# Sharing the low-part subtraction of the split weights between VectorE and GpSimd in a two-block kernel

## The chip, the cores and the metric

The kernel runs on one core of one Trainium2 chip. The metric is device time in microseconds (us) from start to end of one execution. A core has TensorE (PE, matmul), VectorE (DVE), ScalarE (ACT), GpSimd (POOL) and SyncE (SP); here SP only issues the weight transfers.

## The reference

Two transformer-like blocks run over 256 tokens of width 2048, all in float32. The first has a pooling mixer, a gated linear recurrence (RG-LRU) and a product-key expert layer (PEER: 8 heads, top 16 of 128 x 128 experts, gathered rows of `peer_u` and `peer_v`). The second has a stick-breaking attention, a causal depthwise convolution of 31 taps, two gates and an MLP with squared ReLU. Cut to the products that carry the time:

```python
# first block
proj = rmsnorm(x) @ w_in;  y = [pool_mixer(proj), rg_lru(proj)];  h = x + y @ w_out
s1, s2 = q @ keys1.T, q @ keys2.T;  expert = top16 of top16(s1) + top16(s2);  gate = softmax
h = h + sum_k gate_k * gelu(peer_u[expert_k] . z) * peer_v[expert_k]
# second block
q, k, v, glu_a, glu_b, g1, g2 = split(rmsnorm(x) @ w_in_2 + b_in_2)
merged = sigmoid(g1) * (attention(q, k, v) @ w_sb) + sigmoid(g2) * (conv(glu) @ w_cv)
x = x + rmsnorm(merged @ w_o)
x = x + rmsnorm(square(relu(rmsnorm(x) @ w_up)) @ w_down)
```

The expert layer is computed densely: all 16384 rows of `peer_u` and `peer_v` are multiplied, in 8 chunks, and a gate matrix made with one-hot products picks the experts that count.

## The kernel before

**Products in split form.** Every weight product keeps float32 accuracy by splitting both operands into a high part (rounded to fp32r, the fast type of TensorE) and a low part (the rest). The activations stand in `ZA` or `ZB` with 512 columns: 256 high and 256 low. A weight tile of 128 x 128 takes two matmuls: `hi` times all 512 columns, and `lo` times the first 256.

**Units and halves.** The work is a list of `N` = 544 units u. A unit is one block of 128 output rows against 2048 inputs (16 weight tiles), and it comes in two halves of 8 tiles (512 KB of weights each): 1088 halves h, in the order of `HALVES`. The stages by unit number: 0 to 39 the mixer projections (`lx`, `pl`, `gt`, `ot`), 40 to 55 the query product (`wq`), from `UB[0]` = 56 to 311 the expert chunks (`u` and `v`), from `F0` = 312 the second block's projections with attention and convolution between them, 352 to 383 gates, 384 to 399 merge, 400 to 415 output, and from `M0` = 416 the MLP (`up`, `dn`).

**The path of a half.** SP loads it into one of three buffers `raw` (line 338). ACT rounds it into one of five buffers `hi` (line 615). DVE subtracts, `lo = raw - hi`, over 128 x 1024 elements (line 978). PE waits for `lo` and runs 16 matmuls (lines 386 and 387). SP may load the next half into a `raw` buffer when the subtraction that read it is done; this is a wait on `s_lo` in `sync_program`. On PE the wait is `weights_ready`.

**Order on each engine.** ACT, DVE and POOL run the same function `walk(u, evac, prep)` for each unit: `evac` handles the results of the unit before in up to three parts, and between the parts `prep` handles the two halves 2u+3 and 2u+4. On ACT `prep` is the rounding and on DVE the subtraction. On POOL `prep` is an empty function. Each engine runs its program in the written order, so a wait in it holds all that stands behind it.

**Evacuation.** ACT copies the low half of a result out of PSUM (line 622), DVE adds the two halves (`join`, line 984), and POOL scales by the norm (line 1451) or adds a residual (lines 1491, 1524). `join` has one input in PSUM and one in SBUF. The subtraction of line 978 has two inputs in SBUF.

**What runs between.** In units 42 to 59 DVE searches the top 16 (`MAX8`, `MATCH_REPLACE8`, `FIND_INDEX8`). In units 61 to 72 it decodes and picks indices (lines 1211, 1220, 1229), with half of each pick on POOL (line 1587). In units 67 to 82 it makes the one-hot matrices `oneB` and `oneA` (lines 1253, 1255), four per unit; ACT scales half of each `oneB` by the gate (line 787), POOL the other half (line 1595), and PE multiplies them (line 474). In units 314 to 366 DVE runs 248 convolution taps, five per unit (lines 1271 and 1274; two SBUF inputs for most), beside four attention groups whose mask products are on POOL (lines 1621 and 1628).

## Time and profile before

| | us |
|---|---|
| median of 3 runs (3285.91 to 3322.47) | 3305.0 |
| the profiled execution, its own time | 3285.91 |
| its span from first to last instruction | 3283.7 |
| PE busy | 3173.8 |
| DVE busy | 2180.9 |
| ACT busy | 1690.9 |
| POOL busy | 876.5 |

The profile is one execution. Busy time of an engine is the union of its instructions; an instruction that is held up after its start by another engine's use of a shared resource still shows as busy. A timeline row gives start, duration, engine, line, operation, shapes and count; a bracket gives the idle time before it and what ended it. The line numbers are those of the kernel before.

### The profile page before, as it was taken

The numbers are of one execution on the slowest core, as the hardware profiler recorded it, in microseconds if no ns is written. First come the engines' busy times: TensorE is split into PE (matmuls) and PEld (weight loads), VectorE is DVE, ScalarE is ACT, GpSimd is POOL, SyncE is SP. The second block draws the span as 40 slices with busy tenths as digits, with TensorE's granted clock in tenths as the row PEclk, the third lists the DMA queues.
The fourth block names the chain that finished last, engine by engine and source line by source line (L and its number), as shares of the span: only waits on it lengthen the run. The fifth ranks groups of instructions, "written<-read, shape, count | busy, mean of one in ns | idle before, by whom it ended". The sixth has DMA issues, their size and how long they took to land.

```text
span 3283.7 us, 46918 instructions
## 1 busy us (share of the span) xinstructions
PE 3173.8 (97%) x18206; PEld 2776.8 (85%) x18206; DVE 2180.9 (66%) x2875; ACT 1690.9 (51%) x2618; POOL 876.5 (27%) x808
## 2 busy tenths in 40 slices
PE   7999989999999999999999999999998999999997
PEld 6788878888888888888888877888887788888886
DVE  7857998764656555565656579898666855555555
ACT  5554456544545444454545645555656444444454
POOL 2332444531313222231313434323242000000003
PEclk9999999999999999999999999999999999999999
DMA  6465556666666666665666655455665556666664
GB/s 206 144 207 181 167 157 222 226 203 206 188 216 188 217 192 214 190 213 192 212 194 190 187 159 154 154 165 188 187 191 161 158 189 188 190 192 190 190 187 139
DMA packets 177708, 615.35 MB, mean 187 GB/s; under 512 B 18128, under 2 KB 34896, under 8 KB 176080
## 3 DMA queue, kind: packets, MB, share of 16 engines
q1 hardware_dynamic: 157824, 572.59, 55.6%
q10 hardware_dynamic: 19664, 39.76, 3.4%
q8 instruction: 145, 2.38, 0.3%
q14 instruction: 75, 0.61, 0.0%
HBM read 593.41 MB, written 18.87 MB: 186 GB/s over the span
## 4 chain that ended last, share of the span: by engine, by line
PE 73%; DVE 17%; issue 4%; ACT 3%; POOL 2%; DMA 1%; ACTq 0%; POOLq 0%; DVEq 0%
PE G L386 47%; PE G L387 24%; DVE lo L978 7%; DVE CV L1274 2%; DVE oneB L1253 1%; ACT hi L615 1%; POOL tS L1451 1%; DVE tS L984 1%; DVE oneA L1255 1%; ACT oneB L787 0%; DMA raw<-in_pu 0%; DVE ZA L1297 0%; DMA raw<-in_w_in 0%; POOL X L1471 0%; ACT tA L622 0%
## 5 line engine op out<-in xcount | busy, mean ns | idle before, releaser
L386 PE MATMUL G<-ZA,hi 128*128 128x512 f32 x5120 | 1812.5, 398 | 44.0 <-DVE lo L978 26.5
L978 DVE TENSOR_TENSOR lo<-raw,hi 128x1024 fp32r<-128x1024 f32 x1088 | 1429.4, 1333 | 343.0 <-ACT hi L615 342.4
L387 PE MATMUL G<-ZA,lo 128*128 128x256 f32 x5120 | 1435.0, 280 | 0.0
L386 PE MATMUL G<-ZB,hi 128*128 128x512 f32 x3584 | 1250.9, 394 | 5.2 <-DVE ZB L1262 5.2
L615 ACT ACTIVATE hi<-raw 128x1024 fp32r<-128x1024 f32 x1088 | 1119.2, 1052 | 210.0 <-DMA raw<-in_w_in 99.6
L386 PEld LDWEIGHTS G<-ZA,hi 128*128 128x128 f32 x5120 | 966.9, 189 | 271.9 <-DVE lo L978 33.7
L387 PE MATMUL G<-ZB,lo 128*128 128x256 f32 x3584 | 1003.4, 280 | 0.0
L387 PEld LDWEIGHTS G<-ZA,lo 128*128 128x128 f32 x5120 | 972.7, 190 | 0.5
L386 PEld LDWEIGHTS G<-ZB,hi 128*128 128x128 f32 x3584 | 673.1, 188 | 158.7 <-issue 3.5
L387 PEld LDWEIGHTS G<-ZB,lo 128*128 128x128 f32 x3584 | 678.4, 189 | 0.0
L622 ACT ACTIVATE tA<-G 128x256 f32<-128x256 f32 x560 | 212.8, 380 | 898.0 <-PE G L387 893.1
L1451 POOL TENSOR_TENSOR tS<-tS,R 128x256 f32<-128x256 f32 x224 | 258.0, 1152 | 694.5 <-DVE tS L984 694.5
L984 DVE TENSOR_TENSOR tS<-G,tA 128x256 f32<-128x256 f32 x336 | 141.4, 421 | 254.7 <-ACT tA L622 242.0
L1491 POOL TENSOR_TENSOR tA<-tA,X 128x256 f32<-128x256 f32 x128 | 104.9, 819 | 545.8 <-ACT tA L622 545.8
L984 DVE TENSOR_TENSOR X<-G,tA 128x256 f32<-128x256 f32 x128 | 54.4, 425 | 273.0 <-POOL tA L1491 273.0
L1524 POOL TENSOR_TENSOR tA<-tA,Y 128x256 f32<-128x256 f32 x48 | 35.4, 738 | 612.9 <-ACT tA L622 612.9
L984 DVE TENSOR_TENSOR Y<-G,tA 128x256 f32<-128x256 f32 x80 | 34.0, 425 | 168.1 <-POOL tA L1524 128.3
L1487 POOL TENSOR_TENSOR tS<-tS,Gc 128x256 f32<-128x256 f32 x96 | 123.4, 1285 | 50.9 <-ACT tS L655 50.9
L1274 DVE SCALAR_TENSOR_TENSOR CV<-UC,col,CV 128x256 f32<-128x256 f32 x240 | 123.0, 513 | 6.9
L1595 POOL TENSOR_TENSOR oneB<-oneB,IJG 128x512 f32<-128x512 f32 x32 | 62.6, 1956 | 79.6 <-DVE oneB L1253 79.6
L474 PE MATMUL M<-oneB,oneA 128*128 128x128 f32 x512 | 66.9, 286 | 15.7 <-DVE oneA L1255 14.0
L474 PEld LDWEIGHTS M<-oneB,oneA 128*128 128x128 f32 x512 | 62.9, 200 | 20.9 <-DVE oneA L1255 18.3
(263 smaller groups left out, 1375.4 us busy)
## 6 DMA issues: line engine op xcount, KB each, us to landing
raw<-in_pu SPq DMA_DIRECT2D x256, 512.0 KB, 4.1
raw<-in_pv SPq DMA_DIRECT2D x256, 512.0 KB, 4.2
raw<-in_w_in SPq DMA_DIRECT2D x192, 512.0 KB, 3.9
raw<-in_w_up SPq DMA_DIRECT2D x128, 512.0 KB, 4.1
raw<-in_w_down SPq DMA_DIRECT2D x128, 512.0 KB, 4.0
raw<-in_w_out SPq DMA_DIRECT2D x32, 512.0 KB, 4.2
raw<-in_wq SPq DMA_DIRECT2D x32, 512.0 KB, 3.9
g_scratch<-stage ACTq DMA_DIRECT2D x16, 1024.0 KB, 7.1
```

The costliest lines, as they stand in the source:

```text
L386: pe.matmul(G[:, 0:512], hi[w][:, k % 8, :], Z[:, k, :], start=first, stop=False, skip_group_check=True)
L387: m = pe.matmul(G[:, 0:256], lo[w][:, k % 8, :], Z[:, k, 0:256], start=False, stop=last, skip_group_check=True)
L474: t = pe.matmul(M[:, 128 * n:128 * n + 128], oA[k % 2][:, 4 * v + n, :], oB[k % 2][:, 4 * v + n, :], start=True, stop=True, skip_group_che ...
L615: act.activation(hi[w][:, :, :], raw[r][:, :].rearrange("p (k n) -> p k n", k=8), ACT.Copy).then_inc(s_hi, 1)
L622: act.activation(tA[b % 3][:, :], GB[b % 4][:, 256:512], ACT.Copy).then_inc(s_low, 1)
L978: dve.tensor_tensor(lo[w][:, :, :], raw[r][:, :].rearrange("p (k n) -> p k n", k=8), hi[w][:, :, :].bitcast(F32), ALU.subtract).then_inc(s ...
L984: dve.tensor_tensor(dst, GB[b % 4][:, 0:256], tA[b % 3][:, :], ALU.add).then_inc(s_join, 1)
L1274: dve.scalar_tensor_tensor(out=CV[:, j, :], in0=b[:, k:k + 256], scalar=w, in1=CV[:, j, :], op0=ALU.mult, op1=ALU.add).then_inc(s_dw, 1)
L1451: pool.tensor_tensor(b, b, R[:, :], ALU.mult).then_inc(s_scl, 1)
L1487: pool.tensor_tensor(b[:, :], b[:, :], Gc[:, :, i], ALU.mult).then_inc(s_gm2, 1)
L1491: pool.tensor_tensor(t[:, :], t[:, :], X[:, i, :], ALU.add).then_inc(s_vx, 1)
L1595: pool.tensor_tensor(oB[k % 2][:, 4:8, :], oB[k % 2][:, 4:8, :], IJG[:, 2, 8 * k + 4:8 * k + 8].unsqueeze(2).broadcast_to([128, 4, 128]), ...
```

## The change

A function `pool_part(h)` says how many of the 8 weight tiles of half h have their low part computed on POOL: 0 for the units 0 to 2, 5 for the units 42 to 59, 4 for the units 60, 61 and 67 to 83, 7 for half 2*M0+3, and 2 for all other halves. POOL takes the last tiles (`c` to 8), DVE the first. A new semaphore `s_lop` counts POOL's parts, and `POOL_SPLITS[h]` is its count after half h. PE waits for both parts before a half's matmuls, and SP waits for both before it loads over a `raw` buffer. The empty `prep` of POOL's `walk` becomes a real one, so POOL's subtractions stand in its program where DVE's stand in DVE's. Two halves at the border M0 are called from POOL's `evac` and from its mixing loop.

```diff
+def pool_part(h):
+    u = h // 2
+    if h == 2 * M0 + 3:
+        return 7
+    if u < 3:
+        return 0
+    if 42 <= u < UB[0] + 4:
+        return 5
+    if UB[0] + 6 <= u < UB[0] + 11:
+        return 2
+    return 4 if UB[0] + 4 <= u < UB[0] + 28 else 2
+POOL_SPLITS = [sum(pool_part(i) > 0 for i in range(h + 1)) for h in range(NH)]
@@ sync_program
                 if h >= NRAW:
                     sp_.wait_ge(s_lo, h - NRAW + 1)
+                    if POOL_SPLITS[h - NRAW]:
+                        sp_.wait_ge(s_lop, POOL_SPLITS[h - NRAW])
@@ tensor_program
             def weights_ready(h):
                 pe.wait_ge(s_lo, h + 1)
+                if POOL_SPLITS[h]:
+                    pe.wait_ge(s_lop, POOL_SPLITS[h])
@@ vector_program
             def prep(h):
-                r, w = h % NRAW, h % NW
+                r, w, c = h % NRAW, h % NW, 8 - pool_part(h)
                 dve.wait_ge(s_hi, h + 1)
-                dve.tensor_tensor(lo[w][:, :, :], raw[r][:, :].rearrange("p (k n) -> p k n", k=8),
-                                  hi[w][:, :, :].bitcast(F32), ALU.subtract).then_inc(s_lo, 1)
+                dve.tensor_tensor(lo[w][:, 0:c, :], raw[r][:, 0:128 * c].rearrange("p (k n) -> p k n", k=c),
+                                  hi[w][:, 0:c, :].bitcast(F32), ALU.subtract).then_inc(s_lo, 1)
@@ pool_program
+            def prep(h):
+                r, w, c = h % NRAW, h % NW, 8 - pool_part(h)
+                if c < 8:
+                    pool.wait_ge(s_hi, h + 1)
+                    pool.tensor_tensor(lo[w][:, c:8, :], raw[r][:, 128 * c:1024].rearrange("p (k n) -> p k n", k=8 - c),
+                                       hi[w][:, c:8, :].bitcast(F32), ALU.subtract).then_inc(s_lop, 1)
@@ pool_program, evac, before the part of "yo"
+                if u == M0 - 1 and part == 1:
+                    prep(2 * M0 + 3)
@@ pool_program, in the loop over MIX_POOL
+                        if n == 6:
+                            prep(2 * M0 + 4)
@@ pool_program, main loop
+            for h in range(3):
+                prep(h)
             for u in range(N + 1):
-                walk(u, evac, lambda h: None)
+                walk(u, evac, prep)
```

## Rows read from the trace of the kernel before

**Rows 1.** The page: span, and busy time of each engine.
```profile
span 3283.7 us, 46918 instructions
PE 3173.8 (97%) x18206; PEld 2776.8 (85%) x18206; DVE 2180.9 (66%) x2875; ACT 1690.9 (51%) x2618; POOL 876.5 (27%) x808
```

**Rows 2.** Busy time by stretch: stretch, its length, then each engine.
```profile
92.00:150.00 58.00, 51.90 (x276) 44.12 (x275) 52.08 (x70) 30.11 (x49) 25.13 (x17) 0.97 0.43 135
...
390.00:444.00 54.00, 49.20 (x271) 41.97 (x270) 48.31 (x71) 25.43 (x41) 20.32 (x17) 0.97 0.53 161
444.00:604.00 160.00, 145.52 (x965) 131.22 (x964) 144.56 (x113) 105.09 (x242) 81.38 (x49) 0.97 0.62 198
...
740.00:1891.00 1151.00, 1151.00 (x6631) 1010.53 (x6630) 654.36 (x732) 581.54 (x873) 310.51 (x331) 1.00 0.63 200
1891.00:2256.00 365.00, 344.66 (x1921) 297.86 (x1920) 317.31 (x452) 197.73 (x276) 128.62 (x89) 0.98 0.52 161
...
2612.00:3258.00 646.00, 646.00 (x3714) 569.36 (x3714) 359.29 (x463) 299.30 (x431) 51.07 (x61) 1.00 0.60 188
```

**Rows 3.** Waits of PE: who waited for whom, total us, times, longest.
```profile
PE G L386 <- DVE lo L978: 26.5, 14, 10.7
PE M L474 <- DVE oneA L1255: 14.0, 7, 3.3
```

**Rows 4.** Groups of DVE by form: busy us, mean ns of one, idle before.
```profile
L978 DVE TENSOR_TENSOR lo<-raw,hi 128x1024 fp32r<-128x1024 f32 x1088 | 1429.4, 1333 | 343.0 <-ACT hi L615 342.4
...
L1065 DVE TENSOR_TENSOR ZA<-tS,ZA 128x256 fp32r<-128x256 f32 x16 | 6.6, 411 | 0.0
```

**Rows 5.** Timeline of DVE and POOL in the expert stage, steady part.
```profile
1202.81 1.38 DVE L978 TENSOR_TENSOR lo<-raw,hi 128x1024 fp32r<-128x1024 f32 x1 [0.52 <-ACT hi L615]
1204.55 1.45 DVE L978 TENSOR_TENSOR lo<-raw,hi 128x1024 fp32r<-128x1024 f32 x1 [0.36 <-ACT hi L615]
...
1202.37 0.74 POOL L1451 TENSOR_TENSOR tS<-tS,R 128x256 f32<-128x256 f32 x1 [3.00 <-DVE tS L984]
1203.64 1.28 POOL L1487 TENSOR_TENSOR tS<-tS,Gc 128x256 f32<-128x256 f32 x1 [0.53 <-ACT tS L655]
```

**Rows 6.** Timeline of DVE: two subtractions in a row, free and behind POOL.
```profile
387.67 2.36 DVE L978 TENSOR_TENSOR lo<-raw,hi 128x1024 fp32r<-128x1024 f32 x2
...
462.51 4.78 DVE L978 TENSOR_TENSOR lo<-raw,hi 128x1024 fp32r<-128x1024 f32 x2 [0.46 <-ACT hi L615]
```

**Rows 7.** Timeline of one unit in the one-hot stage, DVE, ACT, POOL.
```profile
551.28 2.58 DVE L978 TENSOR_TENSOR lo<-raw,hi 128x1024 fp32r<-128x1024 f32 x2 [0.46 <-ACT hi L615]
553.78 1.21 DVE L1253 TENSOR_TENSOR oneB<-con,IJG 128x1024 f32<-128x1024 f32 x1
...
556.05 2.06 DVE L1253 TENSOR_TENSOR oneB<-con,IJG 128x1024 f32<-128x1024 f32 x1
...
560.68 2.58 DVE L978 TENSOR_TENSOR lo<-raw,hi 128x1024 fp32r<-128x1024 f32 x2 [0.46 <-ACT hi L615]
...
558.14 0.41 ACT L787 ACTIVATE oneB<-oneB,IJG 128x128 f32<-128x128 f32 x1 [1.83 <-DVE oneB L1253]
...
559.34 0.36 ACT L622 ACTIVATE tA<-G 128x256 f32<-128x256 f32 x1
559.60 2.00 ACT L615 ACTIVATE hi<-raw 128x1024 fp32r<-128x1024 f32 x2
...
555.07 1.96 POOL L1595 TENSOR_TENSOR oneB<-oneB,IJG 128x512 f32<-128x512 f32 x1 [3.43 <-DVE oneB L1253]
```

**Rows 8.** Timeline of DVE in the attention stage, no idle before any row.
```profile
2086.09 2.89 DVE L978 TENSOR_TENSOR lo<-raw,hi 128x1024 fp32r<-128x1024 f32 x2
2088.90 2.56 DVE L1274 SCALAR_TENSOR_TENSOR CV<-UC,col,CV 128x256 f32<-128x256 f32 x5
...
2091.71 2.90 DVE L978 TENSOR_TENSOR lo<-raw,hi 128x1024 fp32r<-128x1024 f32 x2
```

**Rows 9.** The same timeline where POOL runs two products per unit.
```profile
1951.54 2.89 DVE L978 TENSOR_TENSOR lo<-raw,hi 128x1024 fp32r<-128x1024 f32 x2
...
1957.65 2.89 DVE L978 TENSOR_TENSOR lo<-raw,hi 128x1024 fp32r<-128x1024 f32 x2
```

More of the change, by code:

```diff
@@ L246, in build @@
         s_gc, s_out = sem("s_gc"), sem("s_out")
-        s_hi, s_lo, s_mm, s_low, s_join, s_scl = (
-            sem(n) for n in ("s_hi", "s_lo", "s_mm", "s_low", "s_join", "s_scl"))
+        s_hi, s_lo, s_lop, s_mm, s_low, s_join, s_scl = (
+            sem(n) for n in ("s_hi", "s_lo", "s_lop", "s_mm", "s_low", "s_join", "s_scl"))
         s_zxh, s_zx, s_zph, s_zp, s_zgh, s_zg, s_zhh, s_zh, s_zah, s_za, s_zuh, s_zu = (
```

## The prediction

> **What bounds the kernel now.** I read the page first: PE is busy 3173.8 of 3283.7 us, DVE 2180.9, POOL 876.5 [rows 1]. So at most the 110 us in which PE stands still can be won, whatever is taken off DVE. Then I read busy time by stretch, to see where these 110 us are. From 740 to 1891 us and from 2612 to 3258 us PE is busy without a gap, 1151 and 646 us [rows 2]; more than half of the kernel is PE work and nothing else. The gaps lie where DVE is loaded most: 92 to 150 us (mixers, DVE 52.1 of 58), 390 to 444 us (decoding the experts, 48.3 of 54), 444 to 604 us (one-hot matrices, 144.6 of 160) and 1891 to 2256 us (attention and convolution, 317.3 of 365) [rows 2]. The list of waits says the same: PE waited for the subtraction only 26.5 us, 14 times, and 14.0 us for the one-hot matrices [rows 3]. The change makes that subtraction shorter on DVE, so at first sight it should win back part of some 40 us.
>
> The question is what POOL's help costs DVE. The timeline of the steady expert stage shows it. POOL runs a product from 1203.64 to 1204.92. A DVE subtraction starts at 1204.55 and takes 1.45 us. The one before it starts at 1202.81, under a POOL product that ends at 1203.11, and takes 1.38 us [rows 5]. Free subtractions take half of 2.36 us each when two follow one another [rows 6]. 1.45 less 1.18 is 0.27, and the overlap was 0.37; 1.38 less 1.18 is 0.20, and the overlap 0.30. POOL pays as well: its product at 1203.64 takes 1.28 instead of 0.74, and DVE held on until 1204.19, which is 0.55 later [rows 5]. Nearly the whole overlap comes back as waiting, on whichever side came second. Two engines that subtract or multiply from SBUF at once therefore take turns. The larger case agrees: two subtractions that take 2.36 us free take 4.78 us when a POOL product of 1024 columns (line 1587) gets between them [rows 6]; that is 2.42 us.
>
> The Trainium skill, page "SBUF — State Buffer", section "Who interferes with whom", states the rule: a DVE instruction with two SBUF inputs contends with a GpSimd instruction that reads SBUF, for a pair of ports that one holds for its whole instruction while the other fully blocks. The trace agrees, within about 0.1 us per instruction [rows 5]. By a rule without this lock the port terms below would be gains of 0.5 us per unit where DVE sets the pace.
>
> **The price of the change, per subtraction.** DVE's side: 1024 columns take about 1.20 us and 256 columns 0.41 us [rows 4, 7], so 256 columns less save 0.26 us, 512 less save 0.53 us and 640 less 0.66 us. POOL's side, as time for which DVE is shut out: for 256 columns 0.53 us (2.89 instead of 2.36 for the pair with one POOL product in it) [rows 6, 8]; for 512 columns at least 0.85 us (2.06 instead of 1.21 with line 1595 in front) [rows 7] and at most half of 2.42, 1.21 us [rows 6]. I take 1.0. The trade is bad at every size: a part of 2 tiles saves 0.26 and costs 0.53; a part of 4 tiles saves 0.53 and costs 1.0.
>
> **Where it is hidden.** In the stretches where PE is busy without a gap, DVE is busy 654 of 1151 us and 359 of 646 us [rows 2]. A unit there is 5.55 us of PE work. Two parts of 2 tiles add 2 x 0.53 and save 2 x 0.26, 0.5 us more on DVE out of 2.4 us free per unit. These are most of the 544 units, and I cost them at nothing. The cover is gone where DVE has under 0.5 us left. The two added waits on SP hold nothing but the next load, and those on PE only matmuls that need the data. In units 42 to 59 POOL takes 5 tiles, but there DVE searches with instructions that need no second input from SBUF, and POOL can run under them; a unit also has 6.0 us for PE. I cost it at nothing, with up to 3 us either way.
>
> **Where it shows.** (1) One-hot stage. The two free-running clocks of this stage are PE's work and a ring through DVE and ACT. The ring: subtractions at 551.28, first `oneB` 553.78, second `oneB` at 556.05 for 2.06 us because POOL's half product is in front, ACT's gate scaling at once at 558.14, its evacuation at 559.34, rounding at 559.60 and the next subtraction at 560.68 [rows 7]. No step of it waits for PE, so its 9.40 us is what paces the unit. With the change the ring has two POOL parts of 4 tiles more (2 x 1.0) and loses 2 x 0.53: plus 1.0 us, between 0.6 and 1.4. It goes round 16 times (units 67 to 82): plus 16 us, between 10 and 22. (2) Attention and convolution. DVE has no idle time here, and its period is 5.62 us (2086.09 to 2091.71) [rows 8] against PE's 5.55; where POOL runs one product more per unit it is 6.11 us (1951.54 to 1957.65) [rows 9]. That is the same price again, 0.5 us for each POOL product of 256 columns, read from the pace itself. The change adds two and saves 0.53: plus 0.53 us per unit. About 39 units are paced by DVE; the others lie at the four attention waits, where DVE idles and catches up. 39 x 0.53 is 20.7 us, less a lead of about 1.5 us (my estimate) that PE can use up in each of four rounds: plus 14.7 us. The attention waits themselves have POOL and DVE steps in a row, and POOL's new parts stand in front of them: plus 3 us, four times one part and its wait. (3) Mixers, 92 to 150 us: 8 units with DVE full, 8 x 0.53, plus 4 us. (4) Decoding, 390 to 444 us: plus 1.5 us; DVE pays for the parts, but its own pick comes before POOL's and not behind it. (5) Around the first expert product POOL's gate products wait behind its two parts, once: plus 1 us. (6) At M0 DVE's piece of half 2*M0+3 shrinks to one tile, which frees the `join` behind it about 0.6 to 1 us earlier. In the mixing loop POOL's last mixing step now stands behind a wait for a rounding that comes late, which costs about the same. With the start of the MLP: plus 1 us. The sum is 16 + 14.7 + 3 + 4 + 1.5 + 1 + 1 = 41 us.
>
> The sum is made on the profiled execution of 3285.9 us, which gives 3327 us. That execution is the fastest of three, and their median is 3305.0, so I give the time on the median's scale: 3305 + 41 = 3346 us, plus 1.2%.
>
> **The rivals.** *The parts are absorbed.* PE has its own floor of about 9.35 us in the one-hot stage, POOL may get its parts in while DVE waits for ACT (0.46 us before each pair [rows 7]), and PE may use more of its lead in the attention stage. Then half of (1) and (2) remains and the rest is noise: 0 to 28 us, about 3320. For it speaks that PE waited only 26.5 us for subtractions in all [rows 3]; against it, that DVE shows no idle time in rows 8. *DVE's relief wins.* The mechanism is the DVE-bound units: if POOL's parts fell into moments in which DVE does not need the ports, a unit would shrink by 0.53 us, in 8 + 39 units, and the first six one-hot units, which are over PE's floor, by 1.05 us. That is 25 + 6, and PE cannot win more than its waits there: about 20 to 30 us, 3280. It decides when the POOL part costs DVE less than 0.26 us, and the only row of that price says 0.53. *POOL becomes the bound.* A one-hot unit on POOL is 4.65 us now. The parts add at least 2 x 1.2 us plus what they wait for DVE, some 2 us: 9.1 us, near the ring. A `raw` buffer is also freed later, by the later of two parts, so loads start later and ACT's rounding with them. If either closes a new ring, another 1 to 1.5 us per unit come on top in 16 + 39 units: plus 90 us, 3395.
>
> **How the numbers follow.** Within 1% is about what a measurement of this kernel cannot tell from no change. Chances: turns on the ports as summed 50%, absorbed 32%, DVE's relief 8%, POOL or loads as bound 10%. The likeliest gives 3346. The range goes down to 3292, into the relief case, and up to 3385, short of the whole last case. Slower by over 1% is above 3338: most of the first case (0.42) and the last (0.10), 0.52. Faster by over 1% needs 33 us of the 110, nearly every wait that DVE has a hand in: 0.06 of the relief case. The rest, 0.42, is within 1%.
>
> **What would show it.** After the change, the periods between pairs of subtractions should be 10.4 us instead of 9.40 in the one-hot stage, and about 6.1 instead of 5.62 and 6.6 instead of 6.11 in the attention stage. DVE's pieces of 768 columns should average over 1.1 us, though they take 0.94 when free. PE's waits for `lo`, now from two engines, should grow from 26.5 to over 45 us. The stretches 740 to 1891 and 2612 to 3258 should keep their length. The prediction is wrong if the ring of the one-hot stage keeps 9.4 us, which would mean that POOL's parts find room, or if the long steady stages lengthen, which would mean a new ring through the `raw` buffers.

## The result and the profile after

The changed kernel takes 3384.4 us (median of 4 runs, 3382.2 to 3389.8), the kernel before 3311.8 us (4 runs on the same chip, 3285.9 to 3322.5). The ratio is 1.024, with a 95% interval of 1.0213 to 1.0266: slower by 72.6 us, where 41 were forecast. The profiled execution of after has a span of 3383.7 us, 100.0 more than the 3283.7 of before. The first thing to explain is why these two differences are not the same either.

The page of after: span, busy time of each engine, the share of each in the chain that ended last, and the groups of the two engines that now subtract.

```profile
span 3383.7 us, 49607 instructions
PE 3216.7 (95%) x18206; PEld 2790.0 (82%) x18206; DVE 2276.3 (67%) x2875; ACT 1691.0 (50%) x2618; POOL 2096.8 (62%) x1890
...
PE 63%; DVE 16%; POOL 9%; ACT 5%; DMA 4%; issue 3%; ACTq 0%; POOLq 0%; SPq 0%; DVEq 0%
...
L999 DVE TENSOR_TENSOR lo<-raw,hi 128x768 fp32r<-128x768 f32 (+3 forms) x1088 | 1349.3, 1253 | 414.9 <-ACT hi L636 413.9
L1474 POOL TENSOR_TENSOR lo<-raw,hi 128x256 fp32r<-128x256 f32 (+2 forms) x1082 | 1339.5, 1245 | 443.1 <-ACT hi L636 442.4
```

DVE gave away a quarter or more of each subtraction, and is busy 95 us longer than before, not shorter [rows 1]. The subtractions took 1429.4 us on DVE [rows 4]. Now they take 1349.3 there and 1339.5 on POOL: DVE was relieved of 80 us and the two together work 1259 us more. The same groups by form, and the waits of PE (who waited for whom, total us, times, longest):

```profile
L999 DVE TENSOR_TENSOR lo<-raw,hi 128x768 fp32r<-128x768 f32 x1007 | 1269.9, 1274 | 374.8 <-ACT hi L636 374.3
L1474 POOL TENSOR_TENSOR lo<-raw,hi 128x256 fp32r<-128x256 f32 x1007 | 1213.4, 1212 | 434.3 <-ACT hi L636 433.5
```

```profile
PE G L407 <- POOL lo L1474: 44.1, 36, 5.8
PE M L495 <- DVE oneA L1276: 25.2, 15, 3.3
...
PE G L407 <- DVE lo L999: 12.5, 3, 10.5
...
PE G L407 <- DVE ZA L1061: 5.2, 1, 5.2
```

A piece of 768 columns takes 0.95 us where nothing stands beside it (below) and 1.27 us in the mean. PE waits 44.1 us for POOL's parts and 12.5 for DVE's, together 56.6 against 26.5 [rows 3]; for the one-hot matrices 25.2 against 14.0.

**Where the 100.0 us lie.** For each trace I took the start of the first matmul of every unit. The table shows the time that a range of units took before and by how much each kernel differs from it, in us, out of one profiled execution each. The kernels e1 to e11 are described under the experiments.

```
units            before | after   e1   e3   e4   e5   e6   e7  e10  e11
0-24   mixers     170.2 |  +0.2 -3.6  0.0 -0.2 +0.4 -0.8  0.0  0.0 +0.8
24-42  split of z 101.2 | +11.3 -0.9 +1.6 +0.1 +1.7 +9.8+24.5 +3.8+10.3
42-58  search      96.5 |   0.0  0.0 +0.2  0.0  0.0  0.0  0.0 +1.8 +1.4
58-67  decoding    57.7 |  +8.9 -1.2 +0.6 -0.1 -0.2 +3.6 -0.4 +7.7 +7.9
67-84  one-hot    176.3 | +15.4-11.5+15.3 -0.6 -0.4 -0.8 -0.4 -1.1 +6.0
84-104            118.7 |  +2.5 -3.6 -2.2 -3.4 -0.6 -1.2 -0.8 +1.1 +4.0
104-312 experts  1159.5 | +14.9 -4.1+15.2+13.1+15.2+16.9+20.2+16.8+12.7
312-317            31.4 |  +0.3 -0.8 -0.1 -0.2  0.0  0.0  0.0 -0.1 +0.3
317-366 attention 323.2 | +21.0-18.0 +1.2 -0.1+22.7 +0.2 +0.3  0.0+20.3
366-384 tail of it103.0 | +10.8 -0.9 +0.5 +1.5 +5.0 +8.0 +0.8 +3.4 +6.6
384-428 to MLP    271.5 | +10.5 -2.6 +2.8 +0.4 -0.2 +3.4 +0.4 +2.0 +9.5
428-543 MLP       637.9 |  +4.2  0.0  0.0 +0.9  0.0  0.0+12.3+12.3 +5.7
```

Four groups can be read off. The one-hot stage (+15.4) and attention (+21.0) carry what was forecast for them. Decoding has +8.9. Some stages that were costed at nothing or next to it have +11.3, +10.8 and +10.5. And the two long steady ranges, in which PE is busy without a gap, are longer by 14.9 and 4.2 us. The last group is another matter than the others: kernels that touch nothing in these ranges (e3, e5, e6, e10) have the same +15 to +17 in the experts, and e7 and e10 have +12.3 in the MLP too.

**Two paces of PE.** Busy time by stretch, for 80 or 100 us inside the steady range; columns: stretch, length, busy us and count of PE, PEld, DVE, ACT, POOL, granted clock, DMA share, GB/s. First before, then after, each with two stretches, then e3, which is the kernel before in this range.

```profile
860.00:940.00 80.00, 80.00 (x463) 70.50 (x462) 48.60 (x55) 41.56 (x64) 24.91 (x25) 1.00 0.66 213
1700.00:1800.00 100.00, 100.00 (x579) 88.15 (x577) 62.05 (x69) 53.68 (x84) 32.58 (x33) 1.00 0.61 190
```

```profile
860.00:940.00 80.00, 80.00 (x455) 69.43 (x454) 55.40 (x56) 42.44 (x67) 58.78 (x55) 1.00 0.57 185
1700.00:1800.00 100.00, 100.00 (x579) 87.45 (x578) 60.64 (x60) 45.79 (x65) 56.91 (x59) 1.00 0.61 193
```

```profile
1700.00:1800.00 100.00, 100.00 (x568) 86.67 (x567) 55.66 (x62) 48.78 (x73) 25.38 (x28) 1.00 0.59 189
```

PE is busy in all of each stretch and the granted clock is 1.00 in all five. Yet it gets through 463 matmuls in 80 us or 455, and 579 in 100 us or 568, 1.8% fewer. By units, one takes either 5.55 or 5.65 us, and a range of tens to hundreds of units keeps to one of the two; it changes over only at a stall or at the edge of a stage or chunk. The steady ranges (units 104 to 311 and 428 to 542, 323 units) hold 15 units of the longer kind in the trace of before and 163 in that of after. At 0.106 us each the 148 more are 15.7 us of the 100.0. The other traces have between 0 (e1) and 322 (e7) of them, whether or not POOL takes part there, so I count them to the execution and not to the change. They also fit the spread of the kernel before, whose runs lie between 3286 and 3325 us: 38 us would be some 360 such units. Its profiled execution, with only 15, was the fastest of its runs.

So the stages lost 84 us by the two traces (100.0 less 15.7), the medians differ by 72.6 us, and 41 us were summed. The 84 divide into 50.9 in the stages that had a term (0.2 mixers, 8.9 decoding, 15.4 one-hot, 2.5 first expert product, 21.0 attention, 2.9 units 415 to 427) and 33.8 in work that was costed at nothing: 11.3 in units 24 to 41, 10.8 in 366 to 383, 7.6 in 384 to 414, and 4.1 at the borders of the expert chunks. The two add up to 84.7, within a microsecond of the 84. The short ranges are not free of chance either. e3, which changes nothing there, has +1.6 in units 24 to 41 and +3.3 in 384 to 414, and unit by unit both are the longer pace again (15 and 31 units). The trace of after has 29 such units in 384 to 414 and that of before none: 3.1 of the 7.6 us. In units 366 to 383 e7a (described below) and e10, without a part there, have +3.4 us, nearly all in one unit (378). So 27 to 31 of the 33.8 us are the change's.

### The profile page after: what moved, and what is told of

Its sections match the earlier page's. It is cut to its first block, busy times and chain, and to the rows that moved or that the text cites. A ratio compares the mean times of both kernels' runs of the same rounds, so it can differ in the third digit from the quotient of the medians.

```text
span 3383.7 us, 49607 instructions
## 1 busy us (share of the span) xinstructions
PE 3216.7 (95%) x18206; PEld 2790.0 (82%) x18206; DVE 2276.3 (67%) x2875; ACT 1691.0 (50%) x2618; POOL 2096.8 (62%) x1890
## 4 chain that ended last, share of the span: by engine, by line
PE 63%; DVE 16%; POOL 9%; ACT 5%; DMA 4%; issue 3%; ACTq 0%; POOLq 0%; SPq 0%; DVEq 0%
PE G L407 42%; PE G L408 21%; DVE lo L999 4%; POOL lo L1474 4%; ACT hi L636 3%; DVE CV L1295 3%; DMA raw<-in_w_in 2%; POOL tS L1479 2%; DVE oneB L1274 2%; DVE tS L1005 1%; POOL tS L1534 1%; DMA raw<-in_pu 1%; DVE oneA L1276 0%; DMA raw<-in_wq 0%; ACT oneB L808 0%
## 5 line engine op out<-in xcount | busy, mean ns | idle before, releaser
L407 PE MATMUL G<-ZA,hi 128*128 128x512 f32 x5120 | 1837.7, 402 | 80.5 <-POOL lo L1474 43.7
L999 DVE TENSOR_TENSOR lo<-raw,hi 128x768 fp32r<-128x768 f32 (+3 forms) x1088 | 1349.3, 1253 | 414.9 <-ACT hi L636 413.9
L1474 POOL TENSOR_TENSOR lo<-raw,hi 128x256 fp32r<-128x256 f32 (+2 forms) x1082 | 1339.5, 1245 | 443.1 <-ACT hi L636 442.4
L1479 POOL TENSOR_TENSOR tS<-tS,R 128x256 f32<-128x256 f32 x224 | 217.4, 971 | 336.3 <-DVE tS L1005 336.1
L1295 DVE SCALAR_TENSOR_TENSOR CV<-UC,col,CV 128x256 f32<-128x256 f32 x240 | 150.6, 628 | 6.8
L495 PE MATMUL M<-oneB,oneA 128*128 128x128 f32 x512 | 70.7, 297 | 27.1 <-DVE oneA L1276 25.2
L1065 DVE TENSOR_TENSOR ZB<-tS,ZB 128x256 fp32r<-128x256 f32 x96 | 91.7, 955 | 0.0
```

The lines of the kernel that those rows point to most:

```text
L407: pe.matmul(G[:, 0:512], hi[w][:, k % 8, :], Z[:, k, :], start=first, stop=False, skip_group_check=True)
L495: t = pe.matmul(M[:, 128 * n:128 * n + 128], oA[k % 2][:, 4 * v + n, :], oB[k % 2][:, 4 * v + n, :], start=True, stop=True, skip_group_che ...
L999: dve.tensor_tensor(lo[w][:, 0:c, :], raw[r][:, 0:128 * c].rearrange("p (k n) -> p k n", k=c), hi[w][:, 0:c, :].bitcast(F32), ALU.subtract ...
L1065: dve.tensor_tensor(ZB[:, i, 256:512], b[:, :], ZB[:, i, 0:256].bitcast(F32), ALU.subtract).then_inc(s_zu, 1)
L1295: dve.scalar_tensor_tensor(out=CV[:, j, :], in0=b[:, k:k + 256], scalar=w, in1=CV[:, j, :], op0=ALU.mult, op1=ALU.add).then_inc(s_dw, 1)
L1474: pool.tensor_tensor(lo[w][:, c:8, :], raw[r][:, 128 * c:1024].rearrange("p (k n) -> p k n", k=8 - c), hi[w][:, c:8, :].bitcast(F32), ALU. ...
```

## The experiments

My theory after the result (theory 1): POOL's part costs because it reads SBUF while DVE wants to, and where PE waits each such part is paid. The rivals: it is the added waits and instructions that cost, or POOL's order. Differences by stage are read from one trace each; ratios come from medians against the kernel before on the same chip. In all kernels that limit the sharing, two lines at the start of `pool_part` return 0 outside a range of units.

**What of POOL's part costs, its presence or its reading.** `e1_write_only` is after with a fill in the place of POOL's subtraction, so it leaves the low parts of those tiles out of the computation:

```diff
-                    pool.tensor_tensor(lo[w][:, c:8, :], raw[r][:, 128 * c:1024].rearrange("p (k n) -> p k n", k=8 - c),
-                                       hi[w][:, c:8, :].bitcast(F32), ALU.subtract).then_inc(s_lop, 1)
+                    pool.memset(lo[w][:, c:8, :].bitcast(F32), 0.0).then_inc(s_lop, 1)
```

> The changed kernel with one thing different: POOL's part of each half is a constant written to the same tiles of lo (so those low parts are left out of the computation) in place of a subtraction. Program order, waits, counts and DVE's shorter piece are the same; POOL reads nothing from SBUF and is quicker. Theory 1 (the engines take turns when both read from SBUF): nearly all of the added 99 us goes; the one-hot ring falls from 10.47 to 8.6 to 9.4 us a unit, the attention pace to PE's 5.55, whole kernel 3265 to 3300 us against 3286 to 3322 before. Rival (the added waits and POOL's place in the order cost the time, whatever POOL does there): more than half of the 99 us stays, 3340 to 3385 us.

Measured: 3260.1 us (3238.4 to 3264.9) against 3311.3, ratio 0.984 (0.980 to 0.987). The groups by form, as above for after:

```profile
L999 DVE TENSOR_TENSOR lo<-raw,hi 128x768 fp32r<-128x768 f32 x1007 | 1011.6, 1019 | 363.7 <-ACT hi L636 362.9
...
L1474 POOL MEMSET lo<- 128x256 f32 x1007 | 309.4, 311 | 679.9 <-ACT hi L636 679.4
```

Every wait, every semaphore and every POOL instruction of after is still there, at the same place, and the kernel is 1.6% faster than before instead of 2.4% slower. DVE's piece takes 1.02 us instead of 1.27. What the fill takes away is the reading, the arithmetic and with them the length of POOL's instruction (0.31 instead of 1.21 us). The median lies 5 us below the 3265 to 3300 us expected.

`e2_relief_alone` leaves the parts out altogether: DVE has its short pieces, POOL does nothing for them, and no one waits for it. Not shown below are one fill of `lo` on POOL at the start and a wait for it in front of DVE's first five subtractions.

```diff
-POOL_SPLITS = [sum(pool_part(i) > 0 for i in range(h + 1)) for h in range(NH)]
+POOL_SPLITS = [0] * NH
...
-                if c < 8:
-                    pool.wait_ge(s_hi, h + 1)
-                    pool.tensor_tensor(...).then_inc(s_lop, 1)
+                pass
```

> DVE's pieces are as short as in the changed kernel, but POOL does nothing for them and nobody waits for it; the low parts of the remaining tiles are left out of the computation. It measures what the relief of DVE is worth with no price paid for it. Theory 1: little, since PE has a floor: 15 to 35 us faster than before. Rival (DVE's load is what the kernel is bound by, and only the way of sharing it is bad): 50 us faster or more.

Measured: 3253.9 us (3237.2 to 3271.9), ratio 0.981 (0.976 to 0.987), 57 us faster on medians. Its span is 31.4 us shorter, with 207 of the longer units against 15; without these 192 (20.4 us) it is 52. The steady pieces take 1.04 us:

```profile
L1001 DVE TENSOR_TENSOR lo<-raw,hi 128x768 fp32r<-128x768 f32 x1007 | 1029.4, 1039 | 364.2 <-ACT hi L636 363.4
```

e2 and e1 do not differ by more than their spread, so the waits and POOL's additional instructions cost nothing measurable. I had expected 15 to 35 us from the relief; with 57 it passes the 50 us that were named for the rival, DVE's load as the bound and only this way of sharing it as bad. That is the other half of the account: DVE's shorter pieces are worth 11.8 us in the one-hot stage and 18.1 in attention, and the sharing turned these into losses of 15.4 and 21.0. Against e1, where the pieces are as short and a fill stands in the place of each part, a part that reads and subtracts therefore cost 27 and 39 us there. That it is the reading and not only POOL's longer instruction is told by DVE's own instructions: pieces of the same shape last 1.27 us beside it and 1.02 beside the fill, no more than beside nothing.

**The stages with a term, one at a time.** `e3_onehot_only`:

```diff
+    if not (67 <= u < 84):
+        return 0
```

> Sharing (4 tiles on POOL) only in the halves of units 67 to 83, none elsewhere. Theory 1: the ring of the one-hot stage is 10.4 to 10.5 us a unit as in the changed kernel, plus 15 us in that stage, and no other stage moves: plus 13 to 20 us in all. Rival (the stage lost time because of what came before it in the changed kernel): the stage keeps 9.4 us a unit.

Measured: 3318.8 us, ratio 1.0027 (1.0004 to 1.0050), 7.5 us on medians where 13 to 20 were expected. The stage takes 15.3 us more, as in after; the other ranges differ mostly by the pace (175 longer units in the experts) and by -2.2 us in units 84 to 103. So the stage is as expected, and the whole kernel is below it. Its period is 10.51 us:

```profile
561.75 2.60 DVE L1001 TENSOR_TENSOR lo<-raw,hi 128x512 fp32r<-128x512 f32 x2 [0.46 <-ACT hi L638]
...
572.26 2.60 DVE L1001 TENSOR_TENSOR lo<-raw,hi 128x512 fp32r<-128x512 f32 x2 [0.46 <-ACT hi L638]
```

`e5_attention_only`:

```diff
+    if not (F0 + 4 <= u < SG + 20):
+        return 0
```

> Sharing (2 tiles on POOL) only in units 316 to 371, none elsewhere. Theory 1 (price of taking turns, 0.53 us a unit where DVE sets the pace): units 317 to 365 take 18 to 22 us longer than before, as in the changed kernel (21.0), nothing else moves: plus 17 to 25 us. Rival (the stage was hurt by what the earlier stages left behind): under 10 us.

Measured: 3334.7 us (3317.9 to 3346.7), ratio 1.0093 (1.0065 to 1.0121), 28.8 us on medians where 17 to 25 were expected. Units 317 to 365 take 22.7 us more, the tail 5.0 (its parts reach to unit 371). Both stages stand by themselves: what they lose has its cause inside them.

**The steady stages.** `e4_steady_only`:

```diff
+    if not (104 <= u < F0 or u >= M0 + 12):
+        return 0
```

> Sharing (2 tiles on POOL) only in units 104 to 311 and from 428 on, where PE is busy without a gap in the kernel before. The prediction cost this at nothing. In the changed kernel these stretches are 19 us longer: 0.69 us at the first product of each of 6 expert chunks, and for the rest units of 5.65 in place of 5.55 us. Theory A (sharing causes both): plus 15 to 20 us here too. Theory B (the chunk borders are caused by sharing, the pace of 5.65 is a state of PE that comes and goes by itself): plus 4 us from the borders, and units at either pace in any proportion, anywhere in the kernel.

Measured: 3308.8 us, ratio 0.9996 (0.9979 to 1.0014). Parts in over 300 units cost nothing that can be measured, though the table shows +13.1 in the experts: that range has 93 of the longer units against 15, which makes 8.3 us. The rest is at the chunk borders. The first unit of each of the six expert chunks takes 6.30 us with parts and 5.60 without, 0.7 us six times.

**The stages I had costed at nothing.** `e6_missed_only`:

```diff
+    if not (24 <= u < 42 or 58 <= u < 67 or 366 <= u < 384 or 400 <= u < 402):
+        return 0
```

> Sharing only where the prediction cost it at little or nothing and the changed kernel lost time: units 24 to 41, 58 to 66, 366 to 383, 400 and 401, with its part sizes. Theory (each of these stages has a ring of its own through POOL, ACT and DVE that had under 0.5 us to spare): plus 11, 9, 11 and 4 us in these stages, 30 to 38 us in all. Rival (these losses come from neighbours or from chance): under 15 us.

Measured: 3324.3 us, ratio 1.0057 (1.0027 to 1.0088). Units 24 to 41, 58 to 66, 366 to 383 and 400 to 414 lose 9.8, 3.6, 8.0 and 3.2 us, 24.6 in all, where 30 to 38 were expected. Of this 1.3 are longer units in 24 to 41 and 1.4 in 400 to 414, and 3.2 us of the tail lie in unit 378, which is as long in e7a and within 0.9 us in e10, without a part there. The decoding does not answer as in after: 3.6 instead of 8.9. `e10_search_decode` has the parts in the search as well:

```diff
+    if not (42 <= u < 67):
+        return 0
```

> Sharing only in units 42 to 66, with the part sizes of the change (5 tiles in the search, 4 in units 60 and 61, 2 in units 62 to 66). In the changed kernel units 58 to 66 take 8.9 us more; with sharing only from unit 58 on they took 3.6 us more. Theory A (POOL's parts of 5 tiles in the search, up to unit 59, make POOL late at the start of the decoding): 7 to 10 us more in units 58 to 66 here, nothing in 42 to 57. Theory B (the rest comes from the stages around it): 3 to 5 us again.

Measured: 3325.7 us, ratio 1.0053 (1.0025 to 1.0080), and +7.7 in the decoding: theory A of this run, that the search's parts make themselves felt at the start of the decoding. They cost the search itself at most 1.8 us. Their size is not what matters: e11, with 2 tiles in place of 5, has +7.9. PE's wait there, in e10 (410 to 450 us) and in after (410 to 446 us):

```profile
PE G L409 <- POOL lo L1476: 6.9, 2, 5.7
```

```profile
PE G L407 <- POOL lo L1474: 5.8, 1, 5.8
```

The timeline of after shows who is late, and it is not POOL, as the theory had it. POOL is idle for 1.50 us, then scales the former unit when DVE's join is done (1.38 us), and the two parts stand behind that. DVE is late against PE: its piece for the second half of unit 60 ends 1.7 us after the unit's first matmul in e10 and in after, 1.5 us ahead of it in e6 and 1.0 ahead in before.

```profile
415.79 2.36 DVE L999 TENSOR_TENSOR lo<-raw,hi 128x768 fp32r<-128x768 f32 x2
...
415.95 1.38 POOL L1479 TENSOR_TENSOR tS<-tS,R 128x256 f32<-128x256 f32 x1 [1.50 <-DVE tS L1005]
417.30 2.20 POOL L1474 TENSOR_TENSOR lo<-raw,hi 128x256 fp32r<-128x256 f32 x2
...
418.07 0.83 DVE L1206 CAST dg<-TP 128x256 f32<-128x256 uint32 x1
```

**A ring that I had not seen.** The largest surprise is units 24 to 41. Timelines of before and of after, DVE:

```profile
262.18 2.36 DVE L978 TENSOR_TENSOR lo<-raw,hi 128x1024 fp32r<-128x1024 f32 x2 [2.26 <-ACT hi L615]
264.46 0.48 DVE L1040 SCALAR_TENSOR_TENSOR ZA<-X,col,ZA 128x256 fp32r<-128x256 f32 x1
...
267.59 2.36 DVE L978 TENSOR_TENSOR lo<-raw,hi 128x1024 fp32r<-128x1024 f32 x2 [2.26 <-ACT hi L615]
```

```profile
264.33 2.38 DVE L999 TENSOR_TENSOR lo<-raw,hi 128x768 fp32r<-128x768 f32 x2 [2.25 <-ACT hi L636]
266.63 0.96 DVE L1061 SCALAR_TENSOR_TENSOR ZA<-X,col,ZA 128x256 fp32r<-128x256 f32 x1
267.51 0.41 DVE L1005 TENSOR_TENSOR tS<-G,tA 128x256 f32<-128x256 f32 x1
...
270.18 2.38 DVE L999 TENSOR_TENSOR lo<-raw,hi 128x768 fp32r<-128x768 f32 x2 [2.25 <-ACT hi L636]
...
264.38 2.93 POOL L1474 TENSOR_TENSOR lo<-raw,hi 128x256 fp32r<-128x256 f32 x2 [0.21 <-ACT hi L636]
```

DVE is idle 2.26 us in each unit, both times in front of the subtractions, so by its busy share there is room. But its idle time is a step of a ring: POOL adds the residual, ACT squares it and then rounds the weights, DVE subtracts and splits z, joins, and POOL adds the next. The ring takes 5.41 us in these rows (262.18 to 267.59), 0.14 less than PE's 5.55, and after the change 5.85 (264.33 to 270.18). The two shortened subtractions last 2.38 us, as long as the whole ones did, because POOL's parts begin at the same moment, and the split of z behind them goes from 0.48 to 0.96 us. The idle time has not changed by more than 0.01 us: it belongs to the wait for the others.

`e7a_ot_only` (parts in units 26 to 41 only, a single run) and `e7_ot_late` (the same, and POOL does its parts only when DVE has split z):

```diff
+    if not (26 <= u < 42):
+        return 0
...
-                walk(u, evac, prep)
+                walk(u, evac, prep if not OT < u <= WQ else lambda h: None)
+                if OT < u <= WQ:
+                    pool.wait_ge(s_zh, u - OT)
+                    for h in split_ahead(u):
+                        prep(h)
```

The second hunk belongs to `e7_ot_late` alone.

> Sharing only in units 26 to 41, POOL's part standing in its order as in the changed kernel. Theory (ring of the mixer's output stage: join on DVE, residual on POOL, square and two roundings on ACT, two subtractions and the split of z on DVE, join again): the split of z takes 0.96 in place of 0.48 us behind POOL's part, the ring goes from 5.40 to 5.85 us a unit, over PE's 5.55, and PE waits about 5 us at unit 40: units 24 to 41 plus 7 to 11 us.

> As the run before, but in units 25 to 40 POOL starts its two parts only when DVE has split z (the last step of the ring), so the same work on both engines is no longer in front of the ring's last step. Theory (the place in the ring costs, not the amount of work): the split of z is back at 0.48 us, the ring under 5.55, units 24 to 41 within 3 us of before. Rival (the amount of POOL's work costs, wherever it stands): plus 7 us or more again.

Measured: e7a loses 9.3 us in units 24 to 41 (3316.6 us in its one run), period 5.84, and the split takes 0.95 us. Of the 9.3 us 1.4 are fourteen units at the longer pace; the rest lies in units 24 (1.6), 40 (4.4) and 41 (1.9), so most of the stage's loss comes from the parts inside it. It also shows PE's wait for z, 4.5 us once, that after has too (5.2):

```profile
PE G L409 <- DVE ZA L1063: 4.5, 1, 4.5
```

e7 should have taken the price out of the ring and stayed within 3 us. It lost 24.5 (3342.6 us in its one run), more than twice as much. Its split of z is back at 0.48 us, but POOL's two parts, now late, stand in front of the next residual add, which is the ring's own next step:

```profile
234.98 0.48 DVE L1063 SCALAR_TENSOR_TENSOR ZA<-X,col,ZA 128x256 fp32r<-128x256 f32 x1
...
235.54 1.42 POOL L1476 TENSOR_TENSOR lo<-raw,hi 128x256 fp32r<-128x256 f32 x2 [5.48 <-DVE ZA L1063]
236.92 0.74 POOL L1501 TENSOR_TENSOR X<-tS,X 128x256 f32<-128x256 f32 x1
...
242.40 1.42 POOL L1476 TENSOR_TENSOR lo<-raw,hi 128x256 fp32r<-128x256 f32 x2 [3.48 <-DVE ZA L1063]
```

```profile
PE G L409 <- POOL lo L1476: 13.4, 12, 3.1
```

The period is 6.86 us. So I had two theories of this stage, and the test of the place went against me: no longer beside the split of z, the same parts cost more by standing in POOL's order. Neither end of this ring has a place for them. What I did not try is POOL's part in the middle, between its two adds.

**Smaller parts.** `e11_two_everywhere`:

```diff
+    if u >= 3:
+        return 2
```

> The changed kernel with 2 tiles on POOL in every half from unit 3 on; so the one-hot stage has 2 in place of 4, the search 2 in place of 5, and half 2*M0+3 has 2 in place of 7. It measures how the price goes with size. Theory (price of a part by its columns, 0.53 us for 256, about 1.05 for 512, less the relief of 0.26 or 0.53): the one-hot ring is 9.9 to 10.0 us a unit, half way between 9.41 and 10.5, and units 67 to 83 take 7 to 9 us more than before, not 15. Rival (each POOL instruction costs the same whatever its size): 10.3 us a unit or more. In all 8 to 14 us faster than the changed kernel.

Measured: 3381.5 us (3370.8 to 3385.0), ratio 1.0235 (1.0185 to 1.0286). The period of the one-hot units is 9.94 us, as expected of half the parts:

```profile
564.91 2.58 DVE L1001 TENSOR_TENSOR lo<-raw,hi 128x768 fp32r<-128x768 f32 x2 [0.46 <-ACT hi L638]
...
574.85 2.58 DVE L1001 TENSOR_TENSOR lo<-raw,hi 128x768 fp32r<-128x768 f32 x2 [0.46 <-ACT hi L638]
```

Units 67 to 83 lose 6.0 instead of 15.4 us, yet the medians of e11 and after differ by 3 us where 8 to 14 were expected, and against the kernel before on its own chip each is slower by about as much (74.5 and 72.6 us). By spans it is 15, of which 6 are 57 units fewer at the longer pace. The intervals of the two ratios overlap, so whether the whole kernel gains is open; that the stage does is seen.

**Two versions of the kernel before that try to win from the same finding.** If a POOL product of 256 columns costs DVE 0.5 us where DVE has none to spare [rows 8, 9], the 16 products that POOL runs there ought to move. `e8_scale_later`, made from before:

```diff
-                if F0 + 4 <= u < F0 + 20:
-                    m = u - F0 - 4
+                if F0 + 56 <= u < F0 + 72:
+                    m = u - F0 - 56
```

> The kernel before, with no sharing, and one POOL product moved: the 16 scalings of X by R3 (line 1614) run in units 368 to 383 and not in units 316 to 331, where DVE sets the pace. Theory (each POOL product that reads SBUF costs a DVE-bound unit 0.5 us, by the pace of 6.11 against 5.62 us): units 317 to 333 take 5 to 8 us less, units 368 to 383 under 3 us more: 3 to 7 us faster than before. Rival (DVE's own load sets the pace of 6.11 there): no change in units 317 to 333.

Measured: units 317 to 365 are 7.9 us shorter, with a period of 5.63 where it was 6.11:

```profile
1967.95 2.89 DVE L978 TENSOR_TENSOR lo<-raw,hi 128x1024 fp32r<-128x1024 f32 x2
...
1973.58 2.89 DVE L978 TENSOR_TENSOR lo<-raw,hi 128x1024 fp32r<-128x1024 f32 x2
```

In the tail, where the products are now, 3.1 us more are spent, all in units 377 and 378; e7a and e10 have 3.4 us more there without any change in it, so it is not shown that the products cost this. The whole kernel takes 3303.9 us against 3307.1, ratio 0.9982 (0.9956 to 1.0008): no difference that this measurement can tell. `e9_both` adds to it that DVE builds the one-hot matrix and its gate factor in one go, so that ACT and POOL have no gate products:

```diff
-                dve.tensor_tensor(oB[k % 2][:, :, :], io, IJG[:, 1, ...]..., ALU.is_equal).then_inc(s_ohb, 1)
+                for n in range(8):
+                    m = dve.tensor_scalar(oB[k % 2][:, n, :], iota, IJG[:, 1, 8 * k + n:8 * k + n + 1],
+                                          IJG[:, 2, 8 * k + n:8 * k + n + 1], ALU.is_equal, ALU.mult)
+                m.then_inc(s_ohb, 1)
```

> The run before, and in the one-hot stage the gate is multiplied in by DVE itself: eight small instructions (compare with the index, times the gate, both as per-partition scalars, one SBUF tensor input) make oneB, so the gate products of ACT (128 of them) and of POOL (32, 512 columns each) are gone. Theory: no POOL product in the ring, oneB no longer waits 0.85 us, and ACT's 1.3 us step is out of it; PE's floor of about 9.1 us is left: units 67 to 83 take 12 to 20 us less than before, the kernel 15 to 27 us less in all. Rival (small instructions cost more than the ring gains: 8 of over 0.3 us each): no gain or a loss in that stage.

The hunks that take the gate products off ACT and POOL are left out here. Measured: 3304.6 us, ratio 0.9997 (0.9970 to 1.0023); the stage gains 1.2 us where 12 to 20 were expected, no more than e10 has (1.1) without touching it. The rival held. Eight small instructions take 2.13 us on DVE where one large one took 1.21 and the shut-out by POOL 0.85 [rows 7], so the price of POOL's help was only exchanged for another:

```profile
546.51 2.13 DVE L1245 TENSOR_SCALAR oneB<-con,IJG 128x128 f32<-128x128 f32 x8
```

No version that computes everything is faster than the kernel before by more than its noise; e8 is the nearest.

## Why the prediction was right in direction and too small

**Right: the price, and the two stages it was read from.** One-hot: forecast +16 us and a period of 10.4, measured +15.4 and a period of 10.5:

```profile
579.78 2.59 DVE L999 TENSOR_TENSOR lo<-raw,hi 128x512 fp32r<-128x512 f32 x2 [0.46 <-ACT hi L636]
582.30 2.31 DVE L1274 TENSOR_TENSOR oneB<-con,IJG 128x1024 f32<-128x1024 f32 x1
584.53 1.21 DVE L1276 TENSOR_TENSOR oneA<-con,IJG 128x1024 f32<-128x1024 f32 x1
585.67 2.06 DVE L1274 TENSOR_TENSOR oneB<-con,IJG 128x1024 f32<-128x1024 f32 x1
...
590.29 2.59 DVE L999 TENSOR_TENSOR lo<-raw,hi 128x512 fp32r<-128x512 f32 x2 [0.46 <-ACT hi L636]
...
580.10 3.42 POOL L1474 TENSOR_TENSOR lo<-raw,hi 128x512 fp32r<-128x512 f32 x2
```

The pair of half-size subtractions takes 2.59 us, as the pair of whole ones did [rows 7]: what was saved went to one POOL part. The other lies across the first `oneB`, which takes 2.31 instead of 1.21. That is the sum's 2 x 1.0 less 2 x 0.53, in the places where it was put. That the stage's total came so near is in part luck: the ring was to go round 16 times at the added price, and only units 74 to 81 run at this period (+8.8 us). The seven before them, at 6 to 16 us each in the trace of before, gain 3.8 us and the last two 2.8.

Attention: forecast 14.7 + 3 us, measured +21.0. Of the two periods forecast one came: 18 pairs of subtractions that followed one another at 5.57 us in the mean before now do so at 6.04, against 6.1. The eight at 6.11 are at 6.33 in the mean, not 6.6: where POOL has a product of its own, the two parts cost 0.22 us and not 0.5. A unit of the first kind:

```profile
2148.38 2.36 DVE L999 TENSOR_TENSOR lo<-raw,hi 128x768 fp32r<-128x768 f32 x2
2150.66 3.39 DVE L1295 SCALAR_TENSOR_TENSOR CV<-UC,col,CV 128x256 f32<-128x256 f32 x5
2154.30 0.95 DVE L999 TENSOR_TENSOR lo<-raw,hi 128x768 fp32r<-128x768 f32 x1
...
2149.89 2.32 POOL L1474 TENSOR_TENSOR lo<-raw,hi 128x256 fp32r<-128x256 f32 x2
```

In the rows one part is paid in the subtractions (2.36 us for a pair that would take 1.9 free) and the rest in the convolution behind them (3.39 for five that took 2.56 [rows 8]). The Trainium skill, page "SBUF — State Buffer", section "Who interferes with whom", has an exclusive lock on a shared port pair for DVE instructions with two SBUF inputs, against POOL instructions that read SBUF and not against those that only write it; e1 and e2 agree with it, since the piece of 768 columns takes 1.02 and 1.04 us beside a fill or nothing, and 1.27 beside a reader.

**Right: the signs to look for.** The piece of 768 columns has a mean of 1.27 us (over 1.1 was named), and PE's waits for `lo` are 56.6 us (over 45). The long steady stretches did not keep their length, which was named as a sign of being wrong through a new ring of the `raw` buffers: they are 19.1 us longer. But 15.7 of it are the pace and 4.1 the chunk borders below, and the rest of their units take 5.55 us as before, so no such ring is seen.

**Wrong: the step "Where it is hidden".** It compared 0.5 us more DVE work with 2.4 us of DVE time free per unit, and costed everything outside six places at nothing. That is true of the steady units (e4: ratio 0.9996) and false of four kinds of place, 33.8 us in all, of which 27 to 31 are left without chance and pace. (a) Units 24 to 41, +11.3: the spare time is no measure where DVE is one step of a ring through POOL and ACT, and that ring had 0.14 us to spare against PE. Its rows were in the trace of before and were not looked at, since PE had hardly a gap there. Of the 11.3 us, 2.5 lie in units 33 to 39, which now run at the ring's pace, 6.4 in units 40 and 41, and 2.5 in unit 24. (b) Units 366 to 383, +10.8: mixing steps of DVE, ACT and POOL in a row at the end of attention, where e6 shows +8.0 by itself. Some 3 us of either may be chance: unit 378 is 3.2 us longer in e7a too. (c) Units 384 to 414, +7.6, of which 3.1 are the pace and 4.5 lie in units 400 and 401, the start of the output product; e6, with parts in these two, has 1.8 there, and e11 6.1. (d) The borders of six expert chunks, 0.69 us each, where PE waits for the first operand, which now ends later:

```profile
PE G L407 <- DVE ZB L1065: 2.5, 6, 0.5
...
L1065 DVE TENSOR_TENSOR ZB<-tS,ZB 128x256 fp32r<-128x256 f32 x96 | 91.7, 955 | 0.0
```

The split `ZB` has a mean of 955 ns; it is 411 free [rows 4].

**Mis-sized: decoding.** 1.5 us were forecast, 8.9 measured. The term left out that DVE enters the decoding late: I costed the search before it at nothing and looked at each stage by itself. e10 less e6 (7.7 less 3.6) says that about 4 us are inherited from the search; the 3.6 are over twice the term by themselves.

**Too high: mixers.** 4 us forecast, 0.2 measured. DVE is full there [rows 2]; why the parts find room in these eight units I did not test. Near the forecast: first expert product 1 (2.5), and the start of the mixing 1 (2.9). The first can't be told from chance, since e3, e4 and e8, which change nothing there, have -2.2 to -3.4 us.

**The floor of the one-hot stage.** 9.35 us were given for PE's own work; in e1 and e2, where DVE is not the limit, a unit takes 9.13 to 9.17. It did not change the sum.

**The scale.** "I give the time on the median's scale" was right, and why it was needed is the pace: the profiled execution of before had 15 of the longer units, and its usual runs, by their times, many more. On the medians the sum is short by 72.6 to 41, on the stages by 84 to 41.

**The rivals.** *Absorbed* (0 to 28 us) is out: one-hot and attention each cost what was summed. *DVE's relief wins* is out as a result, but its size was real: e2, which has the relief without the price, is 57 us faster on medians, twice what was given. *POOL becomes the bound* came about in small: 36 waits of 44.1 us for POOL's parts, and e7, where POOL's order is the ring. It did not come about as forecast, through loads in the one-hot and attention stages.

## What to carry to other kernels

Before work is moved to POOL to relieve DVE, work out the trade per instruction from the trace: here 256 columns gave DVE back 0.26 us and shut it out for 0.5, and no place in this kernel won by it. Where the loss is hidden is not told by an engine's free time but by the slack of each ring it takes part in: follow one unit round all engines in every stage, the ones where PE has no gaps too, and compare the ring with PE's period. And take one execution of both kernels apart by units before a difference of 1% is explained, since between a sixth and a fifth of what two spans showed here (15.7 us in the steady ranges and 3.1 outside) belonged to neither kernel.

## What the runs showed of the hardware

PE has two paces with no gap in its work and the granted clock at 1.00: 5.55 or 5.65 us per unit, 579 or 568 matmul records in 100 us. Steady ranges of 323 units held between 0 and 322 units of the longer kind. It is seen in kernels with and without sharing, changes over only at stalls and stage edges, and makes up to 34 us (322 x 0.106) between executions. What decides it stays open. In the rows above the DMA engines move less at the longer pace (185 and 189 GB/s against 213, 190 and 193), so a heavier load on them is not what slows PE there; the sides of the first comparison lie over different units, though.

A POOL instruction that fills without reading does not disturb DVE's subtractions to speak of: 1.02 us beside it and 1.04 without it, 1.27 beside one that reads (e1, e2 and after).

An instruction of DVE with one input was held up too. The cast of the decoding, which occurs once, takes 0.83 us in the rows above, with POOL's parts beside it. Before it took 0.28:

```profile
400.53 0.28 DVE L1185 CAST dg<-TP 128x256 f32<-128x256 uint32 x1
```

The Trainium skill, page "SBUF — State Buffer", section "Who interferes with whom", also counts copies and casts, in their modes that use two ports, among the instructions that take the shared pair. The longer cast agrees with that; which mode it ran in no trace shows.
